# A transformer block's first attention: where the inverse sums are applied, and who sums up the modulation rows

## The reference, cut to what matters

```
mod_x = silu(c) @ ada_w + ada_b              # ada_w: 1024 x 6144
sh1, sc1, g1, sh2, sc2, g2 = split(mod_x, 6)
...
q: 512 x 8 heads x 96;  k, v: (512 + 256 context) x 8 heads x (96, 64)
s = einsum('bqhd,bkhd->bhqk', q, k) * 96 ** -0.5
p = softmax(s, axis=-1)
o = einsum('bhqk,bkhd->bqhd', p, v)          # 512 x (8 * 64)
...
y = sig(gate_f) * (fourier @ w_fourier) + sig(gate_a) * (o @ w_mla_o)
x = x + g1 * (y @ w_out)
x = x + g2 * mlp(rmsnorm(x) * (1 + sc2) + sh2)
```

## Time and profile before

| | us |
|---|---|
| median of 3 runs (2284.32 to 2285.14) | 2284.89 |
| the profiled execution, by the same clock as the runs | 2280.62 |
| its span in the trace | 2278.8 |

### The profile page before, as it was taken

One profiled execution on the slowest core, in us unless ns is written; L12 is line 12 of the kernel. 1 busy time (PEld: TensorE's weight loads), 2 busy tenths in 40 slices (PEclk: granted clock), 3 DMA queues, 4 the chain that ended last, 5 costly groups with the idle time before them and its releaser, 6 DMA issues.

```text
span 2278.8 us, 28699 instructions
## 1 busy us (share of the span) xinstructions
PE 2189.8 (96%) x11528; PEld 1818.3 (80%) x11528; DVE 890.0 (39%) x1411; ACT 830.4 (36%) x1208; POOL 883.5 (39%) x640
## 2 busy tenths in 40 slices
PE   6999999989999989999999999999999999999998
PEld 3776678878888868979787888887888988888887
DVE  2357945441211237474756410505144244222102
ACT  2455632332322334342434423636234443222212
POOL 0334963434444444032121244131354524444442
PEclk9999989999999999999999999999999999999998
DMA  6411334422223232010211132121232412223221
GB/s 229 156 56 57 126 109 148 148 74 93 93 92 111 93 120 91 13 62 20 92 38 38 38 111 93 45 90 40 105 122 82 153 52 93 92 92 105 98 92 56
DMA packets 179968, 205.89 MB, mean 90 GB/s; under 512 B 3364, under 2 KB 170768, under 8 KB 179472
## 3 DMA queue, kind: packets, MB, share of 16 engines
q1 hardware_dynamic: 176912, 195.17, 26.4%
q10 hardware_dynamic: 2944, 9.15, 1.1%
HBM read 198.01 MB, written 6.29 MB: 90 GB/s over the span
## 4 chain that ended last, share of the span: by engine, by line
PE 80%; POOL 5%; DVE 5%; ACT 2%; issue 1%; DMA 1%; ACTq 0%; DVEq 0%; SPq 0%; POOLq 0%
PE ps L2074 20%; PE ps L2076 20%; PE ps L2075 20%; PE ps L2183 3%; PE ps L2602 2%; POOL raw L708 2%; PE ps L2615 2%; POOL raw L710 2%; POOL w_lo L691 2%; PE ps L2686 2%; PE ps L2703 1%; PE ps L2121 1%; PE ps L2123 1%; PE ps L2122 1%; ACT w_hi L763 1%
## 5 line engine op out<-in xcount | busy, mean ns | idle before, releaser
L691 POOL TENSOR_TENSOR w_lo<-raw,w_hi 128x512 fp32r<-128x512 f32 x586 | 779.8, 1362 | 1331.4 <-ACT w_hi L763 1331.3
L2074 PE MATMUL ps<-h_hi,w_hi 128*128 128x512 f32 x1384 | 559.8, 405 | 13.0 <-DVE h_lo L1413 4.2
L2076 PE MATMUL ps<-h_hi,w_lo 128*128 128x512 f32 x1384 | 544.7, 394 | 0.0
L2075 PE MATMUL ps<-h_lo,w_hi 128*128 128x512 f32 x1384 | 544.0, 393 | 0.0
L763 ACT ACTIVATE w_hi<-raw 128x2048 fp32r<-128x2048 f32 x150 | 285.7, 1905 | 367.1 <-PE ps L2076 359.5
L2074 PEld LDWEIGHTS ps<-h_hi,w_hi 128*128 128x128 f32 x1384 | 262.7, 190 | 74.5 <-issue 10.2
L2076 PEld LDWEIGHTS ps<-h_hi,w_lo 128*128 128x128 f32 x1384 | 262.6, 190 | 56.5
L2075 PEld LDWEIGHTS ps<-h_lo,w_hi 128*128 128x128 f32 x1384 | 263.2, 190 | 52.1 <-issue 1.2
L2074 PE MATMUL ps<-g_hi,w_hi 128*128 128x512 f32 x256 | 99.7, 389 | 0.0
L2076 PE MATMUL ps<-g_hi,w_lo 128*128 128x512 f32 x256 | 99.6, 389 | 0.0
L2075 PE MATMUL ps<-g_lo,w_hi 128*128 128x512 f32 x256 | 99.6, 389 | 0.0
(11 more groups left out here) (417 smaller groups left out, 3817.8 us busy)
## 6 DMA issues: line engine op xcount, KB each, us to landing
raw<-w_in SPq DMA_DIRECT2D x48, 1024.0 KB, 5.2
raw<-w_down SPq DMA_DIRECT2D x27, 1024.0 KB, 5.1
raw<-ada_w SPq DMA_DIRECT2D x24, 1024.0 KB, 5.2
raw<-w_gate_up SPq DMA_DIRECT2D x22, 1024.0 KB, 5.0
raw<-w_up SPq DMA_DIRECT2D x16, 1024.0 KB, 5.4
raw<-w_mkv SPq DMA_DIRECT2D x8, 1024.0 KB, 5.3
raw<-w_out SPq DMA_DIRECT2D x4, 1024.0 KB, 5.2
xT<-bias_band SPq DMA_DIRECT2D x2, 2048.0 KB, 9.8
```

What stands on the lines that cost most here:

```text
L691: ins = nc.gpsimd.tensor_tensor(w_lo[:, split_at[u] % 2, cols], raw[:, u % 2, cols], w_hi[:, split_at[u] % 2, cols].bitcast(F32), ALU.subt ...
L2074: T.matmul(out_, wh, hi, start=start, stop=False, skip_group_check=True)
L2075: T.matmul(out_, wh, lo, start=False, stop=False, skip_group_check=True)
L2076: return T.matmul(out_, wl, hi, start=False, stop=stop, skip_group_check=True)
```

## The change

Three things are changed.

1. In the first attention the probabilities are no longer multiplied by the inverse of their sum. PE transposes them as `expo` leaves them (`turned` waits for `at_exp`). DVE still takes the inverse (`inverse(n)`). On odd n, PE adds, behind the six transposes, one matmul for each head of the pair in the form 128*64: the inverse column, broadcast to 64 columns, against the identity. That leaves, in a free quarter of PSUM bank 5, the inverses along the free axis, in the rows of each head. ACT copies this 128 x 128 to SBUF (`sq2`), ahead of `copy(n)`. Once in eight items DVE multiplies the output 128 x 512 by it (`out_scaled`), ACT takes `out_hi` from the product, and DVE `out_lo`.
2. Each of the twelve modulation units beside the attention is shared out: POOL multiplies tiles 0 to 3 and halves them twice; DVE multiplies and adds tiles 4 to 7 (`share`, one tensor_scalar and three scalar_tensor_tensor of 128 x 256), at items 3, 5, ..., 25; POOL then adds the two rows.
3. The semaphores follow: `ada_by_vector` counts to 12 before the last four units, and SP's and PE's waits with it. The second attention (`kind == "mem"`) is as it was.

The parts of the diff that do this:

```diff
+    SHARE_AT = [2 * a + 3 for a in range(12)]
...
-                nc.gpsimd.tensor_tensor(x, x, over_width(silu_c[:, :, 0], 256), ALU.mult).then_inc(sem["pool_chain"], 1)
-                half(4, x[:, 0:4, :]).then_inc(sem["pool_chain"], 1)
+                low = x[:, 0:4, :]
+                nc.gpsimd.tensor_tensor(low, low, over_width(silu_c[:, 0:4, 0], 256), ALU.mult).then_inc(sem["pool_chain"], 1)
                 half(2, x[:, 0:2, :]).then_inc(sem["pool_chain"], 1)
-                half(1, ada_row_of(a).unsqueeze(1)).then_inc(sem["ada_by_pool"], 1)
+                half(1, x[:, 0:1, :]).then_inc(sem["pool_chain"], 1)
+                pool.wait_ge(sem["pool_chain"], chain + 3)
+                pool.wait_ge(sem["ada_by_vector"], a + 1)
+                nc.gpsimd.tensor_tensor(ada_row_of(a).unsqueeze(1), x[:, 0:1, :], x[:, 4:5, :], ALU.add).then_inc(sem["ada_by_pool"], 1)
...
@@ ACT, in copy(n)
+                    if kind == "one" and n % 2:
+                        g, q = out_group(n)[0], items[n][2]
+                        if g >= 2 and q == 0:
+                            act.wait_ge(sem["at_out_lo"], g - 1)
+                        nc.scalar.activation(sq2[:, g % 2, q * P:(q + 1) * P], ps[:, turned_bank(n) + 1, 2 * P:3 * P], ACT.Copy)
...
@@ ACT, in out_hi(n), called three items late
+                    elif last:
+                        act.wait_ge(sem["at_scaled"], g + 1)
+                        nc.scalar.activation(dst_hi[:, g, :], sq2[:, g % 2, :], ACT.Copy).then_inc(sem["at_out_hi"], 1)
...
@@ DVE
+            def share(a):
+
+                u = ada_units[8 + a]
+                x = raw[:, u % 2, :].rearrange("p (k c) -> p k c", k=KT)
+                dve.wait_ge(w_in_slot[u % 2], load_count[u])
+                dve.wait_ge(sem["c_silu"], 2)
+                link(V.tensor_scalar(x[:, 4, :], x[:, 4, :], silu_c[:, 4, 0:1], None, ALU.mult))
+                for k in range(5, KT):
+                    ins = V.scalar_tensor_tensor(x[:, 4, :], x[:, k, :], silu_c[:, k, 0:1], x[:, 4, :], ALU.mult, ALU.add)
+                    if k < KT - 1:
+                        link(ins)
+                ins.then_inc(sem["ada_by_vector"], 1)
...
+                def inverse(n):
+                    dve.wait_ge(sem["at_exp"], n + 1)
+                    V.reciprocal(at_stat[:, n % 4, 3:4], at_stat[:, n % 4, 2:3]).then_inc(sem["at_prob"], 1)
+
+                def out_scaled(n):
+                    g, last = out_group(n)
+                    if last:
+                        dve.wait_ge(sem["at_out"], n + 1)
+                        V.tensor_tensor(sq2[:, g % 2, :], ps[:, out_bank(n), :], sq2[:, g % 2, :],
+                                        ALU.mult).then_inc(sem["at_scaled"], 1)
...
@@ DVE, in the loop over n
-                    normalise(n)
+                    if kind == "one":
+                        inverse(n)
+                    else:
+                        normalise(n)
                     if n + 2 < b:
                         maximum(n + 2)
-                    if n - 2 >= a:
+                    if kind == "one":
+                        if n - 2 >= a:
+                            out_scaled(n - 2)
+                        if n - 3 >= a:
+                            out_lo(n - 3)
+                        if n in SHARE_AT:
+                            share(SHARE_AT.index(n))
...
@@ PE, in turned(n) and pair_values(n)
-                    pe.wait_ge(sem["at_prob"], n + 1)
+                    if kind == "one":
+                        pe.wait_ge(sem["at_exp"], n + 1)
+                    else:
+                        pe.wait_ge(sem["at_prob"], n + 1)
...
+                    if kind == "one" and n % 2:
+                        pe.wait_ge(sem["at_prob"], n + 1)
+                        for a_ in range(2):
+                            i = n % 4 - 1 + a_
+                            ins = T.matmul(ps[a_ * V1:(a_ + 1) * V1, turned_bank(n) + 1, 2 * P:3 * P],
+                                           at_stat[:, i, 3:4].broadcast_to([P, V1]), con("ident"), start=True, stop=True,
+                                           skip_group_check=True)
                     ins.then_inc(sem["at_turned"], 1)
...
-                        pe.wait_ge(sem["at_out_lo"], g - 1)
+                        pe.wait_ge(sem["at_scaled"], g - 1)
```

More of the change, by code:

```diff
@@ L594, in wait_raw_slot @@
                 else:
[L595 removed]
+                    sp.wait_ge(sem["ada_by_vector"], 12 + BY_VECTOR.index(ada_units.index(u - 2) - 8) + 1)
             def load(u, loop=None, src=None):
@@ L695, in modulate @@
             def modulate(a):
-                u, chain = ada_units[8 + a], 3 * BY_POOL.index(a)
+                u, chain = ada_units[8 + a], 3 * a
                 pool.wait_ge(w_in_slot[u % 2], load_count[u])
@@ L966, in out_hi @@
                     g, last = out_group(n)
-                    if last:
+                    if last and kind == "mem":
                         act.wait_ge(sem["at_out"], n + 1)
[L969 to L974, removed]
+                        for j in range(2):
+                            nc.scalar.activation(dst_hi[:, 2 * (g - 4) + j, :], ps[:, out_bank(n, j), :],
                                                  ACT.Copy).then_inc(sem["at_out_hi"], 1)
+                    elif last:
+                        act.wait_ge(sem["at_scaled"], g + 1)
+                        nc.scalar.activation(dst_hi[:, g, :], sq2[:, g % 2, :], ACT.Copy).then_inc(sem["at_out_hi"], 1)
                 expo(a)
@@ L986, in attention @@
                         expo(n + 2)
-                    if n > a:
-                        out_hi(n - 1)
+                    late = 3 if kind == "one" else 1
+                    if n - late >= a:
+                        out_hi(n - late)
                     if n - a in hi_at:
                         next_hi()
-                out_hi(b - 1)
+                for n in range(b - late, b):
+                    out_hi(n)
             attention("one", prob1, probT1, QK1 ** -0.5, at_hi, (30, 31), lambda: store_qk(9))
@@ L1568, in out_lo @@
                     if kind == "mem":
-                        tiles = [(2 * (g - 4) + j, out_bank(n, j), 4 + 2 * (g - 4) + j) for j in range(2)]
+                        tiles = [(2 * (g - 4) + j, ps[:, out_bank(n, j), :], 4 + 2 * (g - 4) + j) for j in range(2)]
                     else:
-                        tiles = [(g, out_bank(n), g)]
-                    for k, bank, count in tiles:
+                        tiles = [(g, sq2[:, g % 2, :], g)]
+                    for k, src, count in tiles:
                         dve.wait_ge(sem["at_out_hi"], count + 1)
-                        V.tensor_tensor(dst_lo[:, k, :], ps[:, bank, :], dst_hi[:, k, :].bitcast(F32),
+                        V.tensor_tensor(dst_lo[:, k, :], src, dst_hi[:, k, :].bitcast(F32),
                                         ALU.subtract).then_inc(sem["at_out_lo"], 1)
@@ L1579, in attention @@
                 for n in range(a, b):
-                    normalise(n)
+                    if kind == "one":
+                        inverse(n)
+                    else:
+                        normalise(n)
                     if n + 2 < b:
                         maximum(n + 2)
-                    if n - 2 >= a:
+                    if kind == "one":
[5 more added lines that the diff above has]
+                            share(SHARE_AT.index(n))
+                        if n == ADA_ITEM:
+                            modulation(0)
+                    elif n - 2 >= a:
                         out_lo(n - 2)
-                    if kind == "one" and n == ADA_ITEM:
-                        modulation(0)
+                if kind == "one":
+                    out_scaled(b - 2)
+                    out_scaled(b - 1)
+                    out_lo(b - 3)
                 out_lo(b - 2)
@@ L2325, in modulation @@
                 pe.wait_ge(sem["ada_by_pool"], len([a for a in BY_POOL if a < BATCH[b].stop]))
-                pe.wait_ge(sem["ada_by_vector"], len([a for a in BY_VECTOR if a < BATCH[b].stop]))
+                pe.wait_ge(sem["ada_by_vector"], BATCH[b].stop)
                 if b < 2:
```

5 lines of the change are left out of this document (3 added, 2 removed).

## The result

The changed kernel is slower: median 2292.25 us of 13 runs, beside 2284.32 of the kernel before; the ratio is 1.0043, 95% interval 1.0027 to 1.0059, some 9.8 us (the two medians lie 7.9 us apart). One of the 13 runs took 3673 us at a mean granted clock of 0.55; the ratio and its interval leave it out. The prediction had 2287.8 us, with no change to be told as the likeliest (0.6) and slower at 0.3. The median lies in the range of 2281.5 to 2293, but that is luck: the loss is some three times the forecast one and comes from a wait that is not in the prediction. The direction was not the one forecast.

The account below looks back on a forecast made before the run. PE, busy for 96% of the span, was taken to bound the kernel, with DVE only just a bound in the first attention. 2.5 - 0.8 - 1.15 + 2.3 = +2.9 us on 2284.89 gave 2287.8 us, range 2281.5 to 2293.

Parts of the forecast that it names:

- One pair, the price on PE: First attention's twelve pairs: four new matmuls add 0.57 us to PE's 5.60, giving 6.17 a pair, +2.5 us in all.
- One pair, VectorE: DVE in a pair: without the multiplication but with the share it works some 4.1 us, under PE's 5.6.
- Rival C: ACT's copy at odd items, ahead of `pair_values`, becomes the bound: +4.5 us, 2292.3 us; chance 0.17.
- The end of the full stretch: Last `pair_values` to the first modulation matmul: the wait for POOL's tenth unit goes, 4.68 us for 5.83, -1.15 us.
- The modulation: The forty modulation matmuls on PE, 7.52 us before: no change predicted (0).
- rival E: Modulation and tail: the clock stays up, -6.4 us, 2281.4 us; chance 0.11.
- The tail: Behind the modulation: later copies, DVE's product and a contended `out_lo` add 0.73 + 0.28 + 0.72 + 0.6, +2.3 us.
- Rival D: In the pairs, SBUF contention lengthens the share's scalar_tensor_tensor and keeps DVE the bound: +9 us, 2297 us; chance 0.05.

Follow-up runs that it names:

- mod_last: Changed kernel with late out_lo, modulation units whole on POOL, new matmuls ahead of `pair_values` in the idle output bank, both modulation batches behind the attention: ratio 0.9985.
- late_lo: The changed kernel with DVE's `out_lo` one item later and PE's modulation waiting for the scaled output: ratio 0.9994 to the kernel before.
- hi_first: The changed kernel with ScalarE's `out_hi` of three items ago ahead of the copy and the exponential: ratio 1.0010 to the kernel before.
- final: mod_last with the first modulation batch back behind item 27 and the merge's first two `w_hi` behind item 31's copy: ratio 0.9981 to the kernel before.
- no_mm: late_lo without the four matmul instructions of each odd item that spread the inverse sums: ratio 0.9979 to the kernel before.
- beside: late_lo with the four new matmuls directly ahead of `pair_values` and ScalarE's 128 x 128 copy one item later: ratio 0.9992 to the kernel before.
- old_mod_last: The kernel before with only the first modulation batch moved from behind item 27 to behind the attention, in its own bank: ratio 1.0037.

## Why the prediction was wrong

**One pair, the price on PE: right, and a little high.** 6.07 us for a forecast of 6.17, 0.47 for 0.57. PE was the bound, with no wait of L2183 for DVE, and the change of form was paid at each odd item: side by side with their own form the four cost 0.22 (mod_last), apart 0.47. The Trainium skill (TensorEngine Tiling (Array Packing), Key Properties) says that a change of tiling mode drains TensorE; the trace agrees, with 0.25 us between the two.

**One pair, VectorE: the step that failed.** The prediction said that "what it delays is the next maximum", and looked only at the share for things that hold VectorE up. It left out the second new wait on that engine: `out_lo` waits for an `out_hi` that waits for an `out_scaled` of the same engine, and ScalarE has it behind a copy and an exponential. Behind the waiting `out_lo` stands the inverse of an odd item, and for that the new matmuls wait. Rival C was dismissed with "DVE has the odd inverse ready nearly two us before": right for 13 odd items of 16, wrong for the three that follow a group of eight. With the clock that falls after the first two waits this is 7.4 us in the pairs, and with the third 8.5 in all; its removal (late_lo) gave back 11 us of the whole, the last of it in stages behind. Rival C had a wait of this kind on ScalarE's side, in the wrong place and of every item.

**The end of the full stretch.** POOL's tenth unit was no longer waited for, as predicted; the third wait for the inverse, 1.15 us, took the place of the 1.06. In late_lo the modulation begins 4.58 us after the 13th `pair_values`, where 4.68 was forecast.

**The modulation: 2.6 us better than forecast.** 4.90 us instead of 7.52. The clock held for most of it (0.92 in 300:305, where the earlier trace rows have 0.63 in 288.6:297.2) and fell behind it (0.50 in 305:311). This is rival E in part, at a price that the sum did not have; some of what it gave was lost at once, the `pair_values` behind it taking 2.83 us for 2.03.

**The tail: +3.3 for +2.3.** The last product and `out_lo`, on DVE:

```profile
323.62 0.69 DVE L1588 TENSOR_TENSOR sq<-ps,sq 128x512 f32<-128x512 f32 x1 [7.54 <-PE ps L2459]
325.01 1.83 DVE L1608 TENSOR_TENSOR at_lo<-sq,at_hi 128x512 fp32r<-128x512 f32 x1 [0.70 <-ACT at_hi L983]
```

`out_lo` took 1.83 us beside POOL's `w_lo`, of the 0.69 to 2.0 that were bounded, and the sum of the two is 2.5. By parts: +1.49 at item 29 (0.73 forecast; 0.8 of it is the clock named above), +0.17 at item 31 (0.28) and +1.65 at the end (1.32). And PE then started the transform in the lower clock:

```profile
327.08 5.86 PE L2511 MATMUL ps<-dft,f_T 128*128 128x256 f32 x16 [1.73 <-DVE mod L1565]
...
339.62 3.73 PE L2520 MATMUL ps<-dft,f_z 128*128 128x128 f32 x32
```

12.54 us from the one to the other, 10.38 before. The prediction had nothing behind 319 us. Why the clock is lower here stays open. The wait of 1.7 us ahead of it is not enough to tell: in hi_first (first row) and in final (second row) PE waits 2.4 us. In the first the sixteen matmuls run partly in the lower clock, in the second all in the upper one; to the next step they are 12.04 and 10.34 us.

```profile
318.27 5.38 PE L2513 MATMUL ps<-dft,f_T 128*128 128x256 f32 x16 [2.40 <-DVE mod L1567]
...
312.70 3.69 PE L2513 MATMUL ps<-dft,f_T 128*128 128x256 f32 x16 [2.38 <-DVE mod L1570]
```

**Rival D** was right to be put low for the changed kernel: the scalar_tensor_tensor there are nearly as fast as undisturbed ones,

```profile
L1556 DVE SCALAR_TENSOR_TENSOR raw<-raw,silu_c 128x256 f32<-128x256 f32 x33 | 16.8, 508 | 1.2
L1554 DVE TENSOR_SCALAR raw<-raw,silu_c 128x256 f32<-128x256 f32 x12 | 6.9, 577 | 0.0
```

0.508 us for the 0.485 of the earlier trace rows. The tensor_scalar was put at 0.35 and takes 0.577 on the mean: 0.35 undisturbed, up to 0.88 beside POOL. In late_lo, where the shares met POOL more often, D cost 1.1 us in twelve pairs; in no_mm nine pairs are 4.4 us longer in all than the other three, in part by it. The GPSIMD Engine Reference of the Trainium skill (1. Specifications) names two SBUF inputs as what contends; the trace of hi_first agrees, with 2.23 us for an `out_lo` of 0.69.

## What to carry to other kernels

When an edit adds a step that goes from one engine to another and back (scale, round, subtract), write down for each engine what stands directly behind the step that waits, and ask who waits for that; an average slack over the loop says nothing on the one iteration in eight in which the step is taken. A short matmul of another form cost its edges (0.25 us) more than its columns (0.22) here: put it beside its own kind, and look whether another engine takes the gain, as in beside. And before work is moved away from a place, look which load or engine was catching up under it.

## What was not expected of the hardware

The granted clock can fall after a short idle time of PE and nearly double its price: the two waits of about 2 us were each followed by 1.6 to 1.7 us lost in the lower level, 3.35 of the 7.39 us above, while the waits of 0.62 and 1.20 us in hi_first cost 0.69 and 1.27 in their pairs, next to nothing but themselves. It is no rule of the length alone: 2.38 us of waiting ahead of final's transform cost nothing more, as shown above. Forty matmuls of one column took 4.90 us in one kernel and 7.52 in another.

The part ahead of the attention, the same in all kernels, took 204.2 to 211.3 us in twelve profiles. The windows of its first 200 us, from a profile with an early start (beside, 204.25) and from that with the latest (old_mod_last, 211.29):

```profile
0.00:200.00 200.00, 175.79 (x833) 126.54 (x834) 88.87 (x153) 89.90 (x137) 43.84 (x36) 0.98 0.39 131
```

```profile
0.00:200.00 200.00, 176.18 (x798) 124.08 (x799) 85.34 (x140) 85.79 (x131) 44.53 (x36) 0.94 0.39 131
```

The mean granted clock is 0.98 in one and 0.94 in the other, and of the twelve profiles the three that start earliest have 0.97 or 0.98, the three latest 0.94, the others 0.95 to 0.97. So 7 us, as much as the whole effect that was looked for, come and go, for the greater part with the clock of a stage that nobody changed; only a stretch inside the trace, or a ratio over many runs, tells an edit from it.
